# TensorE multiplies ones by ones into an unused PSUM bank at places where it waits, in a fused two-block transformer kernel

## What is computed

```python
# first block
h = x + mixer(rms_norm(x))            # GLA (4 heads, chunked decay) and NSA (8 heads: compressed,
                                      # selected and window attention), side by side
h = h + cross_attn(rms_norm(h), rms_norm(mem))   # 4 heads over 256 memory rows
h = h + peer_ffn(rms_norm(h))         # 8 heads, top 16 of 128x128 experts per token
x = rms_norm(h)                       # norm_final
# second block
h = x + hybrid_mixer(rmsnorm(x))      # HGRN scan and a long convolution (Hyena)
h = h + peer_ffn_2(rmsnorm(h))
y = rmsnorm(h)

def rms_norm(x, g):
    return x * rsqrt(mean(x * x, axis=-1) + 1e-6) * g
def cross_attn(hn, memn, wq, wk, wv, wo):
    q, k, v = hn @ wq * dh ** -0.5, memn @ wk, memn @ wv
    return softmax(q @ k.T) @ v @ wo          # per head
```

## Time and profile before

| | |
|---|---|
| time of three runs | 2786.47 us median (2782.92 to 2790.59) |
| the profiled execution | 2786.32 us; span from first to last instruction 2784.5 us |
| mean granted TensorE clock | 0.927 of full speed |
| busy: PE, PEld, DVE, ACT, POOL | 89%, 80%, 65%, 43%, 29% |
| DMA | 384 MB, 138 GB/s on average |

### The profile page before, as it was taken

The page is one execution under the profiler, slowest core; times in us unless marked ns, Lnnn a source line. Parts: engine busy times, 40 slices in busy tenths (PEclk is TensorE's granted clock), DMA queues, the critical chain, the costliest instruction groups (busy, mean ns, idle before and its releaser), DMA issues.

```text
span 2784.5 us, 39123 instructions
## 1 busy us (share of the span) xinstructions
PE 2477.7 (89%) x16062; PEld 2241.5 (80%) x16062; DVE 1823.4 (65%) x2756; ACT 1189.6 (43%) x1911; POOL 816.5 (29%) x389
## 2 busy tenths in 40 slices
PE   6866978999999999998945598978999999999997
PEld 5855868999999888886945597668999999888885
DVE  4545344987888555556468867264887888655554
ACT  3422334444444444443452236324444444444443
POOL 2011000887666100001016500010777666200000
PEclk8866989999999999998976798989999999999998
DMA  4310424555445566663621143335545444566663
GB/s 160 91 61 23 134 86 129 153 168 158 144 145 150 168 188 187 187 187 120 182 76 46 46 130 114 99 96 161 160 149 160 146 145 147 166 188 189 188 189 106
DMA packets 108568, 384.40 MB, mean 138 GB/s; under 512 B 13007, under 2 KB 16000, under 8 KB 107816
## 3 DMA queue, kind: packets, MB, share of 16 engines
q1 hardware_dynamic: 108392, 381.91, 45.0%
HBM read 380.79 MB, written 1.06 MB: 137 GB/s over the span
## 4 chain that ended last, share of the span: by engine, by line
PE 74%; DVE 19%; ACT 3%; POOL 2%; issue 1%; DMA 0%; SPq 0%; DVEq 0%; POOLq 0%; ACTq 0%
PE psum L349 20%; PE psum L350 20%; PE psum L351 20%; PE psum L1742 4%; PE psum L511 1%; DVE peer_experts L1649 1%; DVE peer_experts L1650 1%; PE psum L2138 1%; DVE peer_experts L1626 1%; DVE peer_experts L1618 1%; PE psum L2355 1%; DVE peer_experts L1620 1%; DVE peer_experts L1615 1%; DVE peer_experts L1623 1%; DVE weight_parts L322 1%
## 5 line engine op out<-in xcount | busy, mean ns | idle before, releaser
L349 PE MATMUL psum<-acts_high,weight_parts 128*128 128x256 f32 x3296 | 971.8, 295 | 74.6 <-DVE weight_parts L322 29.0
L350 PE MATMUL psum<-acts_low,weight_parts 128*128 128x256 f32 x3296 | 944.5, 287 | 0.0
L351 PE MATMUL psum<-acts_high,weight_parts 128*128 128x256 f32 x3296 | 944.0, 286 | 0.0
L317 ACT ACTIVATE weight_parts<-weight_ring 128x1024 fp32r<-128x1024 f32 x702 | 736.4, 1050 | 186.6 <-PE psum L351 183.8
L322 DVE TENSOR_TENSOR weight_parts<-weight_ring,weight_parts 128x1024 fp32r<-128x1024 f32 x450 | 563.7, 1254 | 367.6 <-ACT weight_parts L317 367.5
L328 POOL TENSOR_TENSOR weight_parts<-weight_ring,weight_parts 128x1024 fp32r<-128x1024 f32 x252 | 634.4, 2525 | 334.6 <-ACT weight_parts L317 334.0
L349 PEld LDWEIGHTS psum<-acts_high,weight_parts 128*128 128x128 f32 x3296 | 643.8, 195 | 90.8 <-issue 38.1
L350 PEld LDWEIGHTS psum<-acts_low,weight_parts 128*128 128x128 f32 x3296 | 645.4, 196 | 2.5 <-issue 1.7
L351 PEld LDWEIGHTS psum<-acts_high,weight_parts 128*128 128x128 f32 x3296 | 643.9, 195 | 0.0
L349 PE MATMUL psum<-weight_parts,peer_coef 128*128 128x512 f32 x1024 | 405.8, 396 | 4.0 <-issue 3.9
L350 PE MATMUL psum<-weight_parts,peer_coef 128*128 128x512 f32 x1024 | 405.7, 396 | 0.0
(11 more groups left out here) (377 smaller groups left out, 2471.4 us busy)
## 6 DMA issues: line engine op xcount, KB each, us to landing
weight_ring<-in_peer_down SPq DMA_DIRECT2D x128, 512.0 KB, 3.6
weight_ring<-in_peer_up SPq DMA_DIRECT2D x128, 512.0 KB, 3.5
weight_ring<-in_peer_u SPq DMA_DIRECT2D x128, 512.0 KB, 3.6
weight_ring<-in_peer_v SPq DMA_DIRECT2D x128, 512.0 KB, 4.1
weight_ring<-in_w_in SPq DMA_DIRECT2D x88, 512.0 KB, 3.6
weight_ring<-in_w_out SPq DMA_DIRECT2D x16, 512.0 KB, 3.6
weight_ring<-in_peer_w_q SPq DMA_DIRECT2D x16, 512.0 KB, 3.6
weight_ring<-in_w_in_v SPq DMA_DIRECT2D x10, 512.0 KB, 3.5
```

The costliest lines, as they stand in the source:

```text
L317: q.e.activation(self.high, self.ring, ACT.Copy).then_inc(*self.rounded.once())
L349: q.e.matmul(out, sh, mh, start=first, stop=False)
L350: q.e.matmul(out, sh, ml, start=False, stop=False)
L351: return q.e.matmul(out, sl, mh, start=False, stop=last)
```

## The change

A helper `keep_busy` issues n float32 matmuls of a 128 x 128 matrix of ones by itself into columns 0 to 127 of a bank. A step `KeepBusy` takes a bank from the rotation and does so with n = 18 or 30. Three pipelines call the helper themselves, on bank 7. The results are never read.

```diff
+def keep_busy(c, q, b, n):
+    for _ in range(n):
+        last = q.e.matmul(c.bank(b)[:, 0:P], c.ones[:, :], c.ones[:, :], start=True, stop=True)
+    return last
+
+class KeepBusy(Step):
+    def __init__(self, c, n):
+        self.c, self.n, self.b = c, n, c.take_bank()
+        self.bank_free, self.done = c.bank_free[self.b], c.mark("kept_busy")
+        c.bank_free[self.b] = (self.done,)
+    def tensor(self, q):
+        q.wait_ge(*self.bank_free)
+        keep_busy(self.c, q, self.b, self.n).then_inc(*self.done.once())
...
 class GlaLevel(Step):       # __init__: self.busy = c.bank_free[7]
             ql, kl = g.qq[:, u, :, :], g.kk[:, u, :, :]
+            q.wait_ge(*self.busy)
+            keep_busy(c, q, 7, 4)
             q.wait_ge(self.scaled, *self.bank_free)
...
 class Attend(Step):         # __init__: self.busy = c.bank_free[7] if c.memory_normed else ()
+        if self.busy:
+            q.wait_ge(*self.busy)
+            keep_busy(c, q, 7, 6)
         q.wait_ge(self.weighed, self.biased)
...
 class AttendMemory(Step):   # __init__: self.busy = c.bank_free[7]
+        q.wait_ge(*self.busy)
+        keep_busy(c, q, 7, 6)
         q.wait_ge(self.weighed)
...
         nsa_constants(c, s, ctx)
+        c.plan(KeepBusy(c, 18))
         norm = c.plan(Normalize(c, h, c.gain("norm_mix"), work, tmp[:, :], xn, after=[c.gains_came]))
...
+        c.plan(KeepBusy(c, 30))   # ahead of norm_xattn, of the norm of each expert stage, of norm_mix_g_2
```

## The result

| | before | after |
|---|---|---|
| median (range, runs) | 2786.09 us (2775.19 to 2790.62, 20) | 2792.05 us (2784.00 to 2797.36, 20) |
| profiled execution: time; span | 2786.32; 2784.5 us | 2788.37; 2786.5 us |
| mean granted clock | 0.927 | 0.938 |

The ratio is 1.0025 (95% interval 1.0015 to 1.0034): 6 us slower, which is within the 0.3% that I called no change, and inside the forecast's range. The interval excludes that nothing changed at all. The profiled execution, 2.0 us above that of before, says less than that, and the experiments will show why a single execution can be several us off.

The account below looks back on a forecast made before the run. PE bounds the kernel, 74% of the last-ending chain, with 15% of the span at the lower clock. The terms summed to +3.9 us on the profiled 2786.32, forecast 2790 us, no change; range 2780 to 2801.

Parts of the forecast that it names:

- +1.8, -0.4, +0.3, 0: GLA, four ones before each level: predicted us for pairs one to four; A's ones fall into pauses, the first B's don't.
- First norm: 18 ones fit PE's 5.18 us wait; DVE's pace may lose the clock again; bounds -1.6 and 0, taken -0.5 us.
- Norms: Four norms, 30 ones each: bounds -0.3 and +1.9 us for each, +0.6 taken for the sum of all.
- The rival that ones don't count for the clock: Everywhere: ones neither bring nor keep the clock, 30 run 13.5 us at half clock; 2817 us, chance 0.04.
- In the second pair the pause of 2.80 shrinks to 1.95: GLA, second pair: A's ones shorten PE's pause; -0.6 us if the clock holds, +1.6 if it falls, taken -0.4.
- NSA: Six ones before four transposes: two without a pause cost +2.6 us, one does nothing, the last taken at -0.7.
- Cross attention: Six ones before each of four transposes: +0.9 us taken for the first three sets, -0.7 for the fourth.
- so mostly not: Cross attention, fourth set: 2.9 us of pause remain, so the clock mostly falls; a held clock gives back 2.5 us.
- that transposes don't count as activity: Cross attention: by this rule a lost clock stays down between the ones; first term +2.8, whole sum 2 us higher.
- the trace agrees as far as it goes: Cross attention: the clock did not rise during twelve transposes from 400.59, only 3 us into the scores that followed.
- the clock holds: Rival: the clock holds in nearly every shortened pause of GLA, NSA and cross attention; -5 us, 2781, chance 0.18.
- The third rival: Ones don't bring or keep the clock: 30 end at 464.6, block some 6 us late; +19 at norms, +11.5 elsewhere; chance 0.04.

Follow-up runs that it names:

- norms_only: The changed kernel with only the norms' 18 and four times 30 ones, none in GLA, NSA and cross attention; 2787.01 us, ratio 1.0000 to before.
- waits_only: The changed kernel without ones before GLA's B levels, NSA's first and third transposes, cross attention's second and third; 2776.77 us, ratio 0.9969 to before.
- gla_b_only: The changed kernel with four ones only before level B of each GLA pair, no others; 2799.12 us, ratio 1.0048 to before.
- gla_a_only: The changed kernel with four ones only before level A of each GLA pair, no others; 2776.08 us, ratio 0.9970 to before.
- attention_only: The changed kernel with only the six ones before each of four NSA and four cross attention softmax transposes; 2787.92 us, ratio 1.0005 to before.
- gla_only: The changed kernel with only the four ones before each of the eight GLA levels; 2790.98 us, ratio 1.0004 to before.

## Why the prediction was right, and where its terms were not

The forecast, 2790 us and no measurable change, held for the reason given: PE's list is walked in order, and ones between ready operands are paid. But that the sum was near the result is in part luck, because two errors went against each other. By the profiled execution, with the offset of after against before at the same work:

| place | offset in us, after less before | term of the sum |
|---|---|---|
| first A of GLA | -0.9 | -0.5 |
| second, third, fourth pair, level 0 | +0.6, +2.9, +4.4, +6.5 | +1.8, -0.4, +0.3, 0 |
| NSA, its first set to its last transposes | +6.0 to +7.2 | +2.6 - 0.7 |
| cross attention: first scores, values, product behind them | +7.4, +8.2, +6.3 | +0.9 - 0.7 |
| second block behind the norm of the first expert stage | +6.3 | part of +0.6 |
| end | +2.0 | |

By place that is +7.4 us in GLA where the sum had +1.7, +0.7 in NSA where it had +1.9, and -1.1 in cross attention where it had +0.2. The way from +6.3 down to +2.0 lies in stretches without ones (2.0 us around 1300, 2.7 in the second mixer's levels), where the code is that of before and the clock fell at other times; the median, +6.0, is nearer to the +7.0 of the places with ones.

*First norm.* As feared there: 18 ones held the clock up to 26.28 us, then DVE's pace of one k each 1.07 us let it fall, and it was back at 33.10. The -0.9 is not a gain that can be told: norms_only and waits_only have the same 18 ones and are 0.9 and 0.3 us behind before at this point. The window after:

```profile
26.28:33.10 6.82, 6.18 (x24) 5.23 (x24) 5.56 (x10) 3.91 (x7) 6.82 (x13) 0.50 0.99 296
```

*Norms.* Right in kind and size: the stages behind the four norms came +0.2, 0.0, +0.6 and +0.1 us later than those ahead of them. The 30 ones behind the barrier of the first expert stage took 6.94 us and ended 1 us after the first `acts_low`, and the products then followed DVE (PE, DVE, PE; after):

```profile
457.28 6.94 PE L519 MATMUL psum<-ones 128*128 128x128 f32 x60 [0.58 <-DVEq L612]
...
468.35 0.28 PE L349 MATMUL psum<-acts_high,weight_parts 128*128 128x256 f32 x1
```

```profile
462.45 0.43 DVE L563 TENSOR_TENSOR acts_low<-work,acts_high 128x256 fp32r<-128x256 f32 x1
```

From DVE's first step (457.36) to the second block (468.35) it is 11.0 us, as in the earlier trace rows. norms_only gives 1.0000. The rival that ones don't count for the clock is refuted by the set of the last norm: the clock fell at 1900.19 and was back at 1903.60, while PE did nothing but ones (PE and a window; after):

```profile
1899.33 8.56 PE L519 MATMUL psum<-ones 128*128 128x128 f32 x60 [0.58 <-DVEq L612]
```

```profile
1900.19:1903.60 3.41, 3.41 (x19) 3.41 (x18) 1.88 (x2) 1.45 (x2) 0.00 (x0) 0.50 0.95 329
```

*GLA: the step that failed.* "In the second pair the pause of 2.80 shrinks to 1.95", and -0.4, +0.3 and 0 for pairs two to four. The pause did not shrink, it grew to 4.02 plus 1.05 filled, since I let A's ones shorten a pause whose ends I had held fixed. B's ones of the pair before had pushed its end out by 1.5 us through DVE's copy, counted from A, and its start came 0.8 us sooner, because the products behind B ran at full clock. Pair by pair it was +1.5, +2.3, +1.5, +2.1 instead of +1.8, -0.4, +0.3, 0: the sum's +1.7 became +7.4. Alone and in the median, B's sets cost 12.6 us where four times 0.85 to 1.8 had been my bound, 3.4 to 7.2: the ones take up to 2.07 us, and in gla_b_only more of the work behind them ran at half clock. In after, where A's sets stand too, the clock was low in GLA for 23.9 us against 27.3 in before, and the four sets cost their own length, 7.4 us.

*NSA.* The first set cost its 1.3 us. The third, which I priced at the same, cost nothing in the end: the second transposes had come 7.3 us late and the fourth came 7.2 late, since the pauses behind the third set took its time up. The fourth set won nothing: it shortened the pause to 2.24 us, the transposes took 1.09 us, but the clock fell 0.3 us later all the same, at 292.52:

```profile
291.10 1.09 PE L1165 MATMUL psum<-ident,nsa_s 128*128 128x128 f32 x8 [2.24 <-POOL nsa_s L1222]
```

```profile
292.52:295.93 3.41, 3.41 (x19) 3.41 (x18) 1.23 (x1) 1.74 (x3) 0.00 (x0) 0.50 0.00 0
```

*Cross attention.* +1.2 for the first three sets, against +0.9. The fourth won 2.4 us, 0.5 of them by the start of the values and 1.9 in them, where I had written "so mostly not" and taken -0.7 of the -2.5 that a held clock gives. Both are within their bounds. The clock fell at 408.57, as the second set began, and was back at 411.98, behind that set and four transposes: the set at 411.89 ran at full clock. By the rule of the Trainium skill, page "TensorE: Matmul & The Clock Gate", section "Part 4: PE-mode transpose", that transposes don't count as activity, the clock would have stayed down between the ones, at +2.8 us. This trace doesn't agree with that use of the rule, though most of that stretch were ones. For transposes alone two other profiles show it. In gla_a_only PE had idled 13.83 us and then did twelve transposes of NSA, and the clock was back at 225.82, 0.07 us after the scores behind them had begun:

```profile
222.99 1.11 PE L1163 MATMUL psum<-ident,nsa_s 128*128 128x128 f32 x4 [13.83 <-POOL nsa_s L1220]
223.90 1.91 PE L1158 MATMUL psum<-ident,nsa_s 128*15 128x128 f32 x8
```

In attention_only the same twelve began at 222.67, and the clock was back at 225.43. In before they began at 223.21 and the clock stayed down, as it did over those of the earlier trace rows. So transposes can bring the clock back here, though not each time, and "the trace agrees as far as it goes" was said of a trace in which they happened not to.

*The other error.* The sum counted little from shortened pauses: its negative terms make -2.3, its positive ones +6.2. Measured in medians it is -9.8 for the sets in pauses with those of the norms (waits_only) and +12.6 for B's (gla_b_only); what is missing to the change's +6.0 is +3.2, left for the ready sets of NSA and cross attention. The rival "the clock holds" failed for the change as a whole but lived in half of it. The third rival's price was miscounted: ones that end at 464.6 and 5.1 us of products at half clock put the block 7.8 us late, not some 6. Nothing rests on it, since ones did bring the clock back.

*What stays open.* Most of the ten microseconds that waits_only and gla_a_only win lie, in their profiled executions, in places without ones: gla_a_only is 0.5 us ahead of before at GLA's end, and 9.6 at NSA's last transposes, for the reason that the last section shows. No run tells whether earlier stages shift later ones to a better clock as a rule or whether single profiles only show chance.

## What to carry to other kernels

Matmuls put in to hold TensorE's clock belong only in front of a wait, and as long as that wait less a margin: here they won 0.7% when they filled the pauses, and lost 0.5% when they stood before operands that were already there. A pause's length isn't fixed: before counting on a filler to shorten it, follow what an earlier filler does to the engine that ends it, and to the work that begins it. And a low clock is worth winning back only where the next engine waits for TensorE: the scan went from 0.73 to 0.89 for under 2 us.

## What the runs showed of the hardware

*One kernel, two lengths of NSA.* Behind a pause that ends near 223 us, PE works without a gap. In the profile of before it stayed at half clock through all of it, until 246.18 us; in gla_a_only, with the same instructions there, the clock was back at 225.82. Before, then gla_a_only:

```profile
223.21:246.18 22.97, 22.97 (x83) 15.62 (x84) 7.06 (x8) 4.95 (x6) 2.28 (x2) 0.50 0.01 2
```

```profile
222.41:225.82 3.41, 2.83 (x13) 1.97 (x13) 0.55 (x1) 0.60 (x1) 0.92 (x2) 0.50 0.00 0
225.82:229.23 3.41, 3.41 (x18) 2.39 (x19) 1.40 (x2) 2.35 (x3) 0.00 (x0) 1.00 0.02 5
```

From the transposes behind the pause (223.21 and 222.99) to the last output (302.30 and 294.00) it took 79.1 us in before and 71.0 in gla_a_only. attention_only had the short form too, worth 7.6 us by the end of that stretch, which is why its profile is 7.0 us below that of before while its median is not. A PE that is busy without a gap is thus no proof of full clock: 23 us of it passed at 0.50.

*Spread.* The time at which the clock falls and rises differs from one execution to the next, and with it all stages that hang on it: in the 28 runs of before beside gla_a_only the mean granted clock went from 0.924 (2794.3 us) to 0.935 (2768.2 us). Twelve runs of gla_only lie between 2777.7 and 2797.2 us, so a single profile can mislead about a change of 0.3%: that of attention_only is 7.0 us below before's, its median 0.4 above.

*Price of one.* Four matmuls of ones took 1.05 us at full clock and 2.07 at half, six took 1.50 and 2.73, 30 took 6.94: 0.23 to 0.26 us each at full clock and 0.46 to 0.52 at half, a little above the 0.21 and 0.45 of the earlier trace rows.
